# Moving the activation arena and the weight buffers of a float32r transformer kernel by 64 and 128 bytes in SBUF

## The chip, the cores and the metric

The kernel runs on one core of one Trainium2 chip. The metric is the device time of one execution in microseconds (us). The kernel before was timed three times: median 3365.83 us, lowest 3364.95, highest 3367.11.

## The reference

Two transformer layers follow each other on 256 tokens with a model width of 2048, in float32. The first has four mixers side by side (a gated delta rule, a linear recurrence, a spatial gating unit and a short convolution), then an output product and a feed-forward part with a convolution and GELU. The second has a SwiGLU, two kinds of attention with two branch products and an output product, and a second SwiGLU. Cut to the products with a large weight, which is where nearly all of the arithmetic lies:

```python
# first layer
p = h @ w_in                                   # 2048 -> 44 tiles of 128
y = concat(y_a, y_b, y_c, y_d) @ w_out         # 2048 -> 2048
hid = conv(h @ ffn_up); y = (gelu(gate) * val) @ ffn_down        # 2048 -> 11264, 5632 -> 2048
# second layer
x = x + 0.5 * swiglu(norm(x), w_gate, w_up, w_down)              # 2048 -> 2 x 5632, 5632 -> 2048
proj = norm(x) @ w_in_2                                          # 2048 -> 92 tiles of 128
y = sigmoid(g1) * (o_dil @ w_dil) + sigmoid(g2) * (o_diff @ w_diff)
x = x + y @ w_out_2
x = x + 0.5 * swiglu(norm(x), w_gate, w_up, w_down)
```

## The kernel before

Activations are held transposed: 128 channels on the partitions, 256 tokens along the free axis. A value is held as two halves in float32r, a high part and what is left over, side by side: one activation tile of halves is 2 x 256 elements of 4 bytes, 2048 bytes in each partition. Weights are streamed from memory in chunks of eight 128 x 128 tiles (`KG = 8`, 512 KB, 4096 bytes in each partition) through four slots (`SLOTS = 4`), and each chunk passes three buffers. SyncE's queue loads it into `weights_raw` (`load_chunk`, L266). ScalarE rounds it to `weights_high` (`split_high`, L306). VectorE subtracts that from the raw chunk into `weights_low` (`split_low`, L313). A tile of 128 weights columns is 512 bytes in a partition, and a slot is 4096 bytes.

TensorE then works in pairs of k tiles (`multiply_pair`, L463 and L466). For the two k of a pair it multiplies the high weights with both halves of the activation (512 columns), and after them, for the same two k, the low weights with the high half (256 columns). So the order of the weight loads and matmuls is high, high, low, low, without end, and every matmul has a weight load of its own (PEld in the profile), which runs while the matmul before it streams its activation. Within one product the activation tile moves by 2048 bytes from k to k, and the weight tile by 512. The last two tiles of some products go through `multiply_joined` (L478, L481), which takes the halves in two matmuls of 256 columns.

Which activation buffer a product reads depends on the product. `moving_halves` (over `halves_memory`) serves the input, up and gate products of both layers. `gated_halves` begins where the arena begins and serves the three down products. `gated_branch_halves` begins 28 x 1024 bytes into the arena (output product of the second layer), `branch_halves` 4 x 1024 bytes into it (branch products), and `mixed_halves` 4 x 44 x 260 = 45,760 bytes into it (output product of the first layer).

SBUF tensors are laid out one behind the other in the order in which `Core.__init__` asks for them (L150 to L175): `x_T`, `halves_memory`, a gap, `arena`, a gap, `weights_raw`, `weights_high`, `weights_low`, and then the small buffers. The gaps are tensors that nothing reads or writes. Starts are rounded up to 32 bytes, and the sizes named here are multiples of 32.

The engines run in step by semaphores alone: SyncE waits for `low_ready` before it overwrites a raw slot, ScalarE waits for the load and for TensorE to free the slot, VectorE for ScalarE, TensorE for VectorE. ScalarE, VectorE and GpSimd also take the finished accumulators, scale and activate them.

Of the kernel before, what the change touches and what calls it, by code (L numbers as in the profile page):

```python
# [10 lines left out]
F32 = mybir.dt.float32  # L11
# [6 lines left out]
P = 128  # L18
# [37 lines left out]
class Chain:  # L56


    def __init__(self, eng, sem):
        self.eng, self.sem, self.n = eng, sem, 0  # L60
# [84 lines left out]
class Core:  # L145


    def __init__(self, nc, ctx, d):
        self.nc, self.ctx, self.d = nc, ctx, d
        self.x = self.sb("x_T", [P, KT, S], F32)  # L150

        self.h_at = nc.sbuf_base
        self.x_at = self.h_at - KT * S * 4
        self.h_mem = self.sb("halves_memory", [P, KT, 2, S], F32)
        self.h = self.over(self.h_at, "moving_halves", KT)

        self.sb("before_arena", [P, 32], F32)
        self.arena_at = nc.sbuf_base
        self.arena = self.sb("arena", [P, ARENA_TILES, S], F32)
        self.g_parts = self.over(self.arena_at, "gated_halves", FF_TILES)  # L160
        self.y_parts = self.over(self.arena_at + 28 * S * 4, "gated_branch_halves", KT)
        self.sb("before_weights", [P, 48], F32)
        self.raw = self.sb("weights_raw", [P, SLOTS, KG * P], F32)
        self.high = self.sb("weights_high", [P, SLOTS, KG, P], F32R)
        self.low = self.sb("weights_low", [P, SLOTS, KG, P], F32R)
        self.cross = self.sb("cross_products", [P, 2, S], F32)
        self.z = self.sb("unscaled", [P, 2, S], F32)
        self.sq = self.sb("squares", [P, 2, S], F32)
        self.total = self.sb("squares_total", [P, S], F32)
        self.rs = self.sb("token_scale", [P, S], F32)  # L170
        self.trig = self.sb("trig", [ROPE, 2, S], F32)
        self.lam = self.sb("lam", [P, 3], F32)
        self.vec = self.sb("vectors", [P, N_VECTORS], F32)
        self.const = self.sb("constants", [P, N_CONSTS], F32)
        self.scratch = self.sb("stage_scratch", [P, SCRATCH], F32)  # L175
        self.acc = self.scale_bank = None
        self.first_loaded, self.rest_loaded = self.sem("first_loaded"), self.sem("rest_loaded")
        self.half_high, self.half_low = self.sem("half_high"), self.sem("half_low")
        self.loaded = [self.sem(f"weights_loaded{s}") for s in range(SLOTS)]
        self.x_loaded = [self.sem(f"x_loaded{g}") for g in range(KT // 4)]  # L180
        self.high_ready = self.sem("high_ready")
        self.low_ready = self.sem("low_ready")
        self.full_loaded = [self.sem(f"full_loaded{s}") for s in range(SLOTS)]
        self.full_used, self.full_ready = (self.sem(n) for n in ("full_used", "full_ready"))
        self.y_gained, self.squares_added = self.sem("y_gained"), self.sem("squares_added")
        self.fulls = 0
        self.slots_free = self.sem("slots_free")
        self.acc_free = self.sem("acc_free")
        self.cross_ready = self.sem("cross_ready")
        self.z_free, self.idle_in = self.sem("z_free"), self.sem("idle_in")  # L190
        self.y_scaled = self.sem("y_scaled")
        self.x_ready = self.sem("x_ready")
        self.part_high = self.sem("part_high")
        self.part_low = self.sem("part_low")
        self.squared = self.sem("squared")
        self.squares_used = self.sem("squares_used")
        self.summed = self.sem("summed")
        self.carried = self.sem("carried")
        self.var_ready = self.sem("var_ready")
        self.rooted = self.sem("rooted")  # L200
        self.newton = self.sem("newton")
        self.rs_ready = self.sem("rs_ready")
        self.hidden_free = self.sem("hidden_free")
        self.activated = self.sem("activated")
        self.product_ready = self.sem("product_ready")
        self.g_high = self.sem("g_high")
        self.g_low = self.sem("g_low")
        self.swiglus = 0
        self.pairs = 0
        self.halves = 0  # L210
        self.parts = 0
        self.squares = 0
        self.totals = 0
        self.norms = 0
        self.xs = 0
        self.ys = 0
        self.scaled = 0
        self.chunk = 0
        self.tile = 0
# [3034 lines left out]
```

## Time and profile before

| | |
|---|---|
| Median of three runs | 3365.83 us (3364.95 to 3367.11) |
| Profiled execution | 3365.98 us, span 3364.2 us |
| TensorE matmul (PE) busy | 3345.9 us, 99% |
| TensorE weight load (PEld) busy | 2933.9 us, 87% |
| VectorE (DVE) busy | 2240.1 us, 67% |
| ScalarE (ACT) busy | 1746.2 us, 52% |
| GpSimd (POOL) busy | 533.2 us, 16% |
| Memory traffic | 616.21 MB, mean 183 GB/s |
| Granted TensorE clock | 1.000 of 2.4 GHz |

Matmuls are pipelined and one begins long before the one ahead of it has ended, so a mean duration of 395 ns is no rate. The rate is read from starts: how far apart in time the same step of the loop begins again. Here that step is one pair of k tiles, four matmuls.

### The profile page before, as it was taken

Reading aid. Unit: us, or ns where it says so; the run is one execution under the profiler, and the core shown is the slowest. Engines: PE = TensorE matmul, PEld = TensorE weight load, DVE = VectorE, ACT = ScalarE, POOL = GpSimd, SP = SyncE. Lnnn points to the kernel's source line nnn. Section 1 sums busy time; section 2 is a strip of 40 time slices with the busy share of each in tenths; the row PEclk is TensorE's granted clock in tenths of the full one; section 3 lists DMA queues with packets and bytes.
Section 4 is the critical chain, followed back from the end, with each engine's and each line's share of the span. In section 5 each row is a group of like instructions: output and inputs, shape, how many; then the busy total and the mean of one; then the engine's idle time right before and its main releaser. Section 6 shows DMA issues by size and latency. Waiting matters only on the chain.

```text
span 3364.2 us, 59341 instructions
## 1 busy us (share of the span) xinstructions
PE 3345.9 (99%) x19746; PEld 2933.9 (87%) x19746; DVE 2240.1 (67%) x2874; ACT 1746.2 (52%) x2588; POOL 533.2 (16%) x502
## 2 busy tenths in 40 slices
PE   9999999999999999999999999999999999999999
PEld 8888888888888888888888888888888888888888
DVE  7879587777744566556555599766687655656544
ACT  5555665555544554545444555554565554554443
POOL 0214111111100011111100066511100111111000
PEclk9999999999999999999999999999999999999999
DMA  6534555555566555555566655545556555555665
GB/s 213 163 114 154 184 169 189 190 188 187 188 193 188 178 179 192 189 190 187 187 192 189 219 175 175 189 155 159 171 193 199 190 187 193 188 188 189 186 194 175
DMA packets 176036, 616.21 MB, mean 183 GB/s; under 512 B 20912, under 2 KB 21584, under 8 KB 175568
## 3 DMA queue, kind: packets, MB, share of 16 engines
q1 hardware_dynamic: 175520, 609.84, 56.2%
q10 hardware_dynamic: 432, 5.24, 0.4%
q8 instruction: 53, 0.87, 0.1%
q14 instruction: 31, 0.25, 0.0%
HBM read 610.81 MB, written 4.19 MB: 183 GB/s over the span
## 4 chain that ended last, share of the span: by engine, by line
PE 94%; DVE 3%; issue 1%; ACT 1%; DMA 1%; POOL 0%; DVEq 0%; SPq 0%; POOLq 0%; ACTq 0%
PE acc L463 59%; PE acc L466 30%; DVE weights_low L313 1%; PE ps_wide L392 1%; PE acc L478 1%; ACT weights_high L306 0%; PE ps_narrow L2552 0%; PE ps_wide L2528 0%; PE acc L481 0%; DVE halves_memory L568 0%; DMA weights_raw<-in_w_in 0%; DMA x_T<-in_x 0%; DVE halves_memory L3011 0%; DMA weights_raw<-in_w_diff_branch 0%; PE ps_scale L2933 0%
## 5 line engine op out<-in xcount | busy, mean ns | idle before, releaser
L463 PE MATMUL acc<-moving_halves,weights_high 128*128 128x512 f32 x6304 | 1981.0, 395 | 1.8 <-DVE x_T L2821 1.8
L313 DVE TENSOR_TENSOR weights_low<-weights_raw,weights_high 128x1024 fp32r<-128x1024 f32 (+1 forms) x1172 | 1432.8, 1236 | 719.8 <-ACT weights_high L306 718.6
L306 ACT ACTIVATE weights_high<-weights_raw 128x1024 fp32r<-128x1024 f32 (+1 forms) x1172 | 1209.0, 1033 | 773.1 <-PE acc L466 746.7
L466 PEld LDWEIGHTS acc<-moving_halves,weights_low 128*128 128x128 f32 x6304 | 1185.0, 188 | 269.0
L466 PE MATMUL acc<-moving_halves,weights_low 128*128 128x256 f32 x6304 | 1244.0, 279 | 0.0
L463 PEld LDWEIGHTS acc<-moving_halves,weights_high 128*128 128x128 f32 x6304 | 952.4, 188 | 12.0 <-issue 9.8
L463 PE MATMUL acc<-gated_halves,weights_high 128*128 128x512 f32 x2024 | 628.0, 392 | 0.0
L562 ACT ACTIVATE cross_products<-acc 128x256 f32<-128x256 f32 x503 | 192.9, 383 | 671.2 <-PE acc L466 671.1
L466 PEld LDWEIGHTS acc<-gated_halves,weights_low 128*128 128x128 f32 x2024 | 380.1, 188 | 83.8
L585 POOL TENSOR_TENSOR stage_scratch<-unscaled,token_scale 128x256 f32<-128x256 f32 x260 | 215.2, 828 | 1287.2 <-DVE unscaled L568 807.3
L466 PE MATMUL acc<-gated_halves,weights_low 128*128 128x256 f32 x2024 | 399.4, 279 | 0.0
L568 DVE TENSOR_TENSOR unscaled<-acc,cross_products 128x256 f32<-128x256 f32 x354 | 150.0, 424 | 274.5 <-ACT cross_products L562 274.3
L463 PEld LDWEIGHTS acc<-gated_halves,weights_high 128*128 128x128 f32 x2024 | 306.5, 188 | 0.0
L585 POOL TENSOR_TENSOR arena<-unscaled,token_scale 128x256 f32<-128x256 f32 (+1 forms) x74 | 71.7, 969 | 424.4 <-DVE unscaled L568 424.4
L622 POOL TENSOR_TENSOR squares_total<-squares_total,squares 128x256 f32<-128x256 f32 x56 | 42.4, 758 | 524.7 <-ACT squares L609 524.7
L1281 ACT ACTIVATE gated_halves<-stage_scratch 128x256 f32 (+1 forms) x88 | 36.8, 418 | 84.5 <-DVE stage_scratch L1314 84.5
L463 PE MATMUL acc<-gated_branch_halves,weights_high 128*128 128x512 f32 x256 | 79.4, 392 | 0.0
L1187 DVE SCALAR_TENSOR_TENSOR arena<-stage_scratch,vectors,arena 128x256 f32<-128x256 f32 x88 | 63.6, 723 | 21.8 <-ACT arena L1148 20.2
L463 PE MATMUL acc<-mixed_halves,weights_high 128*128 128x512 f32 x240 | 75.5, 396 | 0.3 <-DVE mixed_halves L1966 0.3
L2910 POOL TENSOR_TENSOR arena<-arena,trig 32x512 f32<-32x512 f32 x20 | 75.5, 3776 | 0.0
L463 PE MATMUL acc<-branch_halves,weights_high 128*128 128x512 f32 x192 | 61.3, 401 | 1.0 <-DVE halves_memory L568 0.7
L466 PEld LDWEIGHTS acc<-gated_branch_halves,weights_low 128*128 128x128 f32 x256 | 48.1, 188 | 10.5
(384 smaller groups left out, 2010.7 us busy)
## 6 DMA issues: line engine op xcount, KB each, us to landing
weights_raw<-in_w_in SPq DMA_DIRECT2D x268, 512.0 KB, 3.9
weights_raw<-in_ffn_up SPq DMA_DIRECT2D x176, 512.0 KB, 4.5
weights_raw<-in_ffn_w_gate SPq DMA_DIRECT2D x176, 512.0 KB, 4.1
weights_raw<-in_ffn_w_up SPq DMA_DIRECT2D x176, 512.0 KB, 4.7
weights_raw<-in_ffn_w_down SPq DMA_DIRECT2D x160, 512.0 KB, 4.0
weights_raw<-in_ffn_down SPq DMA_DIRECT2D x80, 512.0 KB, 4.0
weights_raw<-in_w_out SPq DMA_DIRECT2D x64, 512.0 KB, 4.3
weights_raw<-in_ffn_w_down SPq DMA_DIRECT2D x32, 256.0 KB, 2.7
```

What stands on the lines that cost most here:

```text
L306: core.nc.scalar.activation(core.high[:, slot, k0:nk, :].rearrange("p a b -> p (a b)"), core.raw[:, slot, k0 * P:nk * P], ACT.Copy).then_i ...
L313: core.nc.vector.tensor_tensor(core.low[:, slot, k0:nk, :].rearrange("p a b -> p (a b)"), core.raw[:, slot, k0 * P:nk * P], core.high[:, s ...
L392: last = core.nc.tensor.matmul(core.full_sums[:, t, 0:S], w, operand.full[:, k, :], start=(k == 0), stop=(k == KT - 1))
L463: core.nc.tensor.matmul(acc[:, t % 2, :, :], core.high[:, u % SLOTS, k, :], parts[:, prod.first[t] + k0 + k, :, :], start=(k0 + k == 0), s ...
L466: core.last = core.nc.tensor.matmul(acc[:, t % 2, 0, :], core.low[:, u % SLOTS, k, :], parts[:, prod.first[t] + k0 + k, 0, :], start=False ...
L562: core.nc.scalar.activation(core.cross[:, t % 2, :], acc[:, t % 2, 1, :], ACT.Copy).then_inc(core.cross_ready, 1)
L568: core.nc.vector.tensor_tensor(out, acc[:, t % 2, 0, :], core.cross[:, t % 2, :], ALU.add).then_inc(core.acc_free, 1)
L585: core.nc.gpsimd.tensor_tensor(out, core.z[:, t % 2, :], core.rs[:, :], ALU.mult).then_inc(core.z_free, 1)
L622: core.nc.gpsimd.tensor_tensor(core.total[:, :], core.total[:, :], core.sq[:, t % 2, :], ALU.add).then_inc(core.squares_used, 1)
L1187: nc.vector.scalar_tensor_tensor(conv[:, t, :], hidden[:, t, PAD - 1:PAD - 1 + S], tap(i, t, 1), conv[:, t, :], ALU.mult, ALU.add).then_in ...
L1281: nc.scalar.activation(g_parts[:, i, 0, :], g, ACT.Copy).then_inc(core.g_high, 1)
L2910: nc.gpsimd.tensor_tensor(here, here, each(trig[:, 0, :]), ALU.mult).then_inc(pool_own, 1)
```

## The change

The gap of 128 bytes ahead of the arena goes. The gap of 192 bytes ahead of the weight buffers stays. A gap of 192 bytes is put between `weights_high` and `weights_low`. No instruction is added, removed or moved in the program. By the order of the tensors, `arena`, `weights_raw` and `weights_high` start 128 bytes lower than before, and `weights_low` and all that follows it 64 bytes higher. `x_T` and `halves_memory` stay.

```diff
         self.h_mem = self.sb("halves_memory", [P, KT, 2, S], F32)
         self.h = self.over(self.h_at, "moving_halves", KT)
 
-        self.sb("before_arena", [P, 32], F32)
         self.arena_at = nc.sbuf_base
         self.arena = self.sb("arena", [P, ARENA_TILES, S], F32)
         self.g_parts = self.over(self.arena_at, "gated_halves", FF_TILES)
@@
         self.sb("before_weights", [P, 48], F32)
         self.raw = self.sb("weights_raw", [P, SLOTS, KG * P], F32)
         self.high = self.sb("weights_high", [P, SLOTS, KG, P], F32R)
+        self.sb("before_low", [P, 48], F32)
         self.low = self.sb("weights_low", [P, SLOTS, KG, P], F32R)
```

## Rows read from the trace of the kernel before

**Rows 1.** The page, part 1 (busy time by engine) and part 4 (chain).

```profile
PE 3345.9 (99%) x19746; PEld 2933.9 (87%) x19746; DVE 2240.1 (67%) x2874; ACT 1746.2 (52%) x2588; POOL 533.2 (16%) x502
...
PE 94%; DVE 3%; issue 1%; ACT 1%; DMA 1%; POOL 0%; DVEq 0%; SPq 0%; POOLq 0%; ACTq 0%
```

**Rows 2.** Waits of TensorE, longest first: total us, times, longest.

```profile
PE ps_narrow L2453 <- DVE stage_scratch L2425: 2.6, 1, 2.6
```

**Rows 3.** Groups of TensorE instructions, forms apart: count, busy us, mean ns, idle.

```profile
L463 PE MATMUL acc<-moving_halves,weights_high 128*128 128x512 f32 x6304 | 1981.0, 395 | 1.8 <-DVE x_T L2821 1.8
...
L463 PE MATMUL acc<-gated_halves,weights_high 128*128 128x512 f32 x2024 | 628.0, 392 | 0.0
...
L463 PE MATMUL acc<-gated_branch_halves,weights_high 128*128 128x512 f32 x256 | 79.4, 392 | 0.0
L463 PE MATMUL acc<-mixed_halves,weights_high 128*128 128x512 f32 x240 | 75.5, 396 | 0.3 <-DVE mixed_halves L1966 0.3
L463 PE MATMUL acc<-branch_halves,weights_high 128*128 128x512 f32 x192 | 61.3, 401 | 1.0 <-DVE halves_memory L568 0.7
```

**Rows 4.** Windows, PE with moving_halves: stretch, us, busy, matmuls, clock, DMA.

```profile
1200.00:1660.00 460.00, 460.00 (x2656) 1.00 0.57 189
```

**Rows 5.** The same with gated_halves alone.

```profile
3130.00:3330.00 200.00, 200.00 (x1162) 1.00 0.63 190
```

**Rows 6.** Timeline of a product with moving_halves: start us, length us.

```profile
1500.22 0.62 PE L463 MATMUL acc<-moving_halves,weights_high 128*128 128x512 f32 x2
...
1500.45 0.42 PEld L466 LDWEIGHTS acc<-moving_halves,weights_low 128*128 128x128 f32 x2
...
1500.69 0.39 PE L466 MATMUL acc<-moving_halves,weights_low 128*128 128x256 f32 x2
...
1500.81 0.30 PEld L463 LDWEIGHTS acc<-moving_halves,weights_high 128*128 128x128 f32 x2
...
1500.92 0.62 PE L463 MATMUL acc<-moving_halves,weights_high 128*128 128x512 f32 x2
```

**Rows 7.** Timeline of a product with gated_halves.

```profile
1000.25 0.62 PE L463 MATMUL acc<-gated_halves,weights_high 128*128 128x512 f32 x2
...
1000.49 0.42 PEld L466 LDWEIGHTS acc<-gated_halves,weights_low 128*128 128x128 f32 x2
...
1000.72 0.39 PE L466 MATMUL acc<-gated_halves,weights_low 128*128 128x256 f32 x2
...
1000.83 0.30 PEld L463 LDWEIGHTS acc<-gated_halves,weights_high 128*128 128x128 f32 x2
...
1000.94 0.62 PE L463 MATMUL acc<-gated_halves,weights_high 128*128 128x512 f32 x2
...
1001.17 0.42 PEld L466 LDWEIGHTS acc<-gated_halves,weights_low 128*128 128x128 f32 x2
...
1001.40 0.40 PE L466 MATMUL acc<-gated_halves,weights_low 128*128 128x256 f32 x2
...
1001.52 0.30 PEld L463 LDWEIGHTS acc<-gated_halves,weights_high 128*128 128x128 f32 x2
...
1001.63 0.62 PE L463 MATMUL acc<-gated_halves,weights_high 128*128 128x512 f32 x2
```

**Rows 8.** Timeline of the product with mixed_halves, three pairs of k apart.

```profile
400.33 0.63 PE L463 MATMUL acc<-mixed_halves,weights_high 128*128 128x512 f32 x2
...
402.42 0.63 PE L463 MATMUL acc<-mixed_halves,weights_high 128*128 128x512 f32 x2
```

**Rows 9.** All engines in an up product: busy us and count of PE, PEld, DVE, ACT, POOL.

```profile
1200.00:1660.00 460.00, 460.00 (x2656) 403.55 (x2655) 274.89 (x333) 229.19 (x332) 66.92 (x83) 1.00 0.57 189
```

**Rows 10.** Groups of instructions in the stretch 1200 to 1660 us.

```profile
L313 DVE TENSOR_TENSOR weights_low<-weights_raw,weights_high 128x1024 fp32r<-128x1024 f32 x167 | 212.8, 1291 | 114.3 <-ACT weights_high L306 114.3
...
L306 ACT ACTIVATE weights_high<-weights_raw 128x1024 fp32r<-128x1024 f32 x166 | 175.3, 1056 | 50.7 <-PE acc L466 47.0
```

## The prediction, before the changed kernel had run

> **What bounds the kernel now.** The page comes first: matmuls cover 99% of the span and TensorE holds 94% of the chain that ended last [rows 1]. The waits of TensorE come next: the longest in the whole run is 2.6 us, and it occurs once [rows 2]. So in the large products TensorE waits for no other engine, and the time is the number of matmuls by the distance between their starts. The groups of instructions give the number: 6304 matmuls of high weights read `moving_halves`, 2024 `gated_halves`, 256 `gated_branch_halves`, 192 `branch_halves` and 240 `mixed_halves` [rows 3]. Two of them, with their two of low weights, are one pair of k tiles, which I use as the unit: 3152 pairs with `moving_halves`, 1012 + 128 + 96 = 1236 with the three buffers that begin at the arena's start or a multiple of 512 bytes behind it, 120 with `mixed_halves`.
>
> Now the distance. With `moving_halves`, 460 us hold 2656 matmuls, about one and a half of them only cut by the edges (each is recorded as 390 ns long, and one starts every 173 ns): 460 / (2654.5 / 4) = 0.693 us for a pair [rows 4]. With `gated_halves`, 200 us hold 1162, or 1160.5 without the edges: 0.689 us, and the timeline gives 1.38 us for two pairs, 0.690 [rows 5, 7]. With `mixed_halves` three pairs take 2.09 us, 0.697 [rows 8]. The instructions are the same in the three cases, the shapes are the same, the clock is 1.00 in the rows that show it (the upper level, 2.4 GHz), and nothing waits. What differs is where in SBUF the activation tile lies against the weight tile. The pattern of starts repeats whether ScalarE and VectorE are busy or not, so I take the difference to lie between TensorE's own two reads: the activation that it streams and the weights that it loads for the next matmul at the same time (a PEld row begins together with a matmul in each gap [rows 6, 7]).
>
> **Distances.** Tiles move by multiples of 512 bytes in both streams, so what stays the same throughout a product is the distance modulo 512 from the activation tile to the weight tile. Before, from `moving_halves` to `weights_high`: 32,768 + 128 + 94,208 + 192 + 16,384 = 143,680, which is 320 modulo 512. From `gated_halves`: 94,208 + 192 + 16,384 = 110,784, which is 192 (also for the two branch buffers, whose offsets 28,672 and 4096 are multiples of 512). From `mixed_halves`: 110,784 - 45,760 = 65,024, which is 0. `weights_low` lies 16,384 further, so it has the same distance as the high weights in every product. The trace therefore holds three measured points: distance 320 gives 0.693, 192 gives 0.690, 0 gives 0.697.
>
> After: the 128 bytes go, so `moving_halves` has 192 to the high weights; `gated_halves` and its kin keep 192, since arena and high weights move together. `weights_low` is 192 further in all of them: 384. `mixed_halves` has 0 to the high and 192 to the low weights. So 4388 of the 4508 pairs will run in one and the same arrangement, high at 192 and low at 384, and have one pitch P. The change as a whole comes down to P.
>
> **Part 1: high weights.** At 192 they stand as with `gated_halves` now. A weight load of the high tile runs in the gap from the first high matmul to the second and in that from the second low one to the next high one. With `gated_halves` two pairs give 0.24 + 0.11 and 0.23 + 0.11, so 0.345 us for a pair. With `moving_halves` it is 0.23 + 0.11 = 0.34 [rows 6, 7]. Starts are read to 10 ns, so these halves are good to some 5 to 10 ns; their sum is exact by the windows.
>
> **Part 2: low weights.** They load in the gaps from high to low and from low to low: with `moving_halves` 0.24 + 0.12 = 0.36 us, with `gated_halves` 0.23 + 0.11 and 0.23 + 0.12, so 0.345 [rows 6, 7]. What `moving_halves` pays more than `gated_halves` thus lies with the low loads. Distance 384 isn't in the trace. I bound the half from both sides by the cheapest and the dearest half read: 0.34 and 0.36. I take 0.345, the low loads' own value with `gated_halves`, as it is also the nearest to the middle of what three of the four halves show (0.34, 0.345, 0.345). By distance alone the nearest point would be 320, which speaks for more, and this is the weak place of the sum.
>
> **Sum.** P = 0.345 + 0.345 = 0.690. `moving_halves`: 3152 x (0.690 - 0.693) = -10.1 us with the difference unrounded (460 / 663.6 = 0.6932). `gated_halves` and kin: 1236 x 0 = 0. `mixed_halves`: 120 pairs, high still at 0, low now at 192; half of 0.007 each, -0.4 us. Together -10.5 us on the profiled execution's 3365.98 us: 3355.5, so 3355 us. That execution lies 0.15 us from the median of the runs shown, so the same number stands for the median; 1.8 us of it lies outside the span, and the change doesn't touch it. The bounds of P are 0.34 + 0.345 = 0.685 and, above, 0.697, the dearest pitch that the trace has for a whole product. A nanosecond of P is 4.4 us of time, and the time stays as it is at P = 0.692.
>
> **What may move elsewhere, and is costed at nothing.** The raw, high and low buffers are also read and written by ScalarE, VectorE and the loads. In an up product ScalarE is busy 229 and VectorE 275 of 460 us [rows 9]; a split takes 1056 and 1291 ns, and VectorE's idles 114 us there for ScalarE, ScalarE's 47 us for TensorE [rows 10]. A chunk of eight k tiles comes every 4 x 0.693 = 2.8 us, so a split may grow by some 40% before TensorE would wait. If the cover were gone, each 100 ns by which a chunk is late would cost 0.1 us for each of 1172 chunks. The loads come with 0.57 of the DMA engines' time [rows 4], with nothing waiting for them. The stages between the products have under 6% of the chain [rows 1]; their operands move with the arena, and 1% more on all of them is 2 us. I set both at 0.
>
> The skill's rule speaks against the whole sum. The Trainium skill, "SBUF — State Buffer", section "Who interferes with whom", says that only the port pair shared by VectorE and GpSimd causes contention and that TensorE never waits for anyone, its two reads being independent. By that rule no layout could alter a pitch, and the time would stay at 3366 us. This case's trace disagrees: 0.690, 0.693 and 0.697 for the same instructions. A rule on the rate, in "TensorE: Matmul & The Clock Gate", section "Back-to-back issue gap", gives N / 2.4 + 2.5 ns for a matmul taken by itself; 2 x 215.8 + 2 x 109.2 is an estimate of 0.650 us for a pair, so some 40 ns of each pair would be left to win, far more than any distance in the trace has given back.
>
> **The rivals.**
>
> *Better than any row.* The low loads at 384 cost less than the cheapest half read, because high and low no longer meet the activation at the same distance and the delay of one doesn't carry into the other. For it: the pitch with `gated_halves` isn't even, low to low takes 0.68 us and then 0.70 [rows 7], so shorter pairs do occur. Against it: the three distances seen lie within 7 ns. At P = 0.685: 3152 x -8.2 ns = -26 us and 1236 x -5 ns = -6 us, so 3334 us; in this case values from 3325 to 3348.
>
> *Nothing in sum.* Low loads at 384 behave as those at their nearest row, 320, and take away what the high ones give: P = 0.691 to 0.694, which is -6 to +7 us; at 0.692, 3366 us. The same time comes if the layout has no effect of its own and the three pitches have another cause, such as the place in the loop over k; against that, all buffers go through the same loop.
>
> *Slower.* One mechanism: the low loads at 384 run into the stream as they do at 0, modulo 512 the other neighbour, where the whole product shows 0.697 [rows 8]. All down products then lose what they have now, and the up products lose too. At P = 0.696: 3152 x 2.8 = 8.8 us and 1236 x 6 = 7.4 us, so 3382 us. It decides from P = 0.694 on. For it: 384 lies between 320 and 512, the two dearer of the three points. Against it: the low loads' half at 0 isn't known to be the dear one.
>
> **How the numbers follow.** What a measurement of this kernel can tell from no change is about 0.2%, 6.7 us. Forecast (P about 0.690, its own range 3348 to 3360): 0.33. Better than any row: 0.22. Nothing in sum: 0.21, the layout without effect among it. Slower: 0.24. So faster by over 0.2% has 0.33 + 0.22 = 0.55, less 0.01 for values of the forecast near the edge, 0.54; same 0.22; slower 0.24. The range goes from 3332 us, which leaves out a third of the better case (0.08), to 3380 us, which leaves out half of the slower one (0.12).
>
> **What would show it.** In the profile after, counts of instructions and waits are as before, and the pitch of the up and down products is one and the same number; that is the step on which all rests. If the up and down products still differ, the distance modulo 512 isn't what counts. If both show 0.690, part 2 is right; if they agree on another number, part 2 is mis-sized and the time follows at 4.4 us for a nanosecond. If the high loads' gaps (first high to second high, low to high) with `moving_halves` don't come to 0.345, part 1 is wrong. The prediction as a whole is wrong if TensorE's waits grow or if splits take a different time and the matmuls wait for them.

## The result and the profile after

The changed kernel takes 3410.18 us (median of four runs, 3409.53 to 3411.21) against 3365.61 us for the kernel before in the same comparison: a ratio of 1.0129, 95% interval 1.0116 to 1.0143. It is slower by 44.6 us. The forecast was 3355 us, faster, with a range up to 3380 us. Direction and range are both missed.

The page after has the same counts of instructions and the same chain as before [rows 1]; what has grown with the span is TensorE's busy time, by 49 us for the matmuls and 25 us for the weight loads.

```profile
span 3409.4 us, 59341 instructions
PE 3394.8 (100%) x19746; PEld 2958.5 (87%) x19746; DVE 2243.0 (66%) x2874; ACT 1745.1 (51%) x2588; POOL 532.3 (16%) x502
PE 94%; DVE 3%; issue 1%; ACT 1%; DMA 1%; POOL 0%; DVEq 0%; SPq 0%; POOLq 0%; ACTq 0%
```

TensorE's longest wait in the run after is even shorter than the one of before [rows 2]:

```profile
PE acc L463 <- DVE x_T L2821: 1.6, 1, 1.6
```

The windows give the pitch, here with the matmuls on `moving_halves` alone (stretch, us, busy us, matmuls, granted clock, DMA share, GB/s). About one and a half matmuls of each count are cut by the edges, so the pitch of a pair of k tiles is length x 4 / (count - 1.5), as in [rows 4]:

```profile
500.00:900.00 400.00, 400.00 (x2267) 1.00 0.57 186
1250.00:1650.00 400.00, 400.00 (x2277) 1.00 0.58 186
```

That is 0.706 us in the first layer's up product and 0.703 in the second layer's first one, where [rows 4] had 0.693. With `gated_halves`, where [rows 5] had 0.689 and [rows 7] 0.690, the first, the third and the second down product, in this order:

```profile
960.00:1140.00 180.00, 180.00 (x1021) 1.00 0.63 185
...
3190.00:3360.00 170.00, 170.00 (x969) 1.00 0.64 187
1710.00:1890.00 180.00, 180.00 (x1026) 1.00 0.60 184
```

In the order of the rows that is 0.706, 0.703 and 0.703. Up and down products now have the same two values, the granted clock stays at 1.00, and the matmuls only begin further apart. The product with `mixed_halves` went the same way. Two rows of it, four pairs apart:

```profile
399.81 0.63 PE L463 MATMUL acc<-mixed_halves,weights_high 128*128 128x512 f32 x2
...
402.64 0.63 PE L463 MATMUL acc<-mixed_halves,weights_high 128*128 128x512 f32 x2
```

That is 2.83 us for four pairs. The mean over all 120 pairs of this product is 0.706 us, where the trace before has 0.697. The timeline of the second up product, beside [rows 6]:

```profile
1299.65 0.63 PE L463 MATMUL acc<-moving_halves,weights_high 128*128 128x512 f32 x2
1299.88 0.42 PEld L466 LDWEIGHTS acc<-moving_halves,weights_low 128*128 128x128 f32 x2
1300.12 0.40 PE L466 MATMUL acc<-moving_halves,weights_low 128*128 128x256 f32 x2
1300.23 0.30 PEld L463 LDWEIGHTS acc<-moving_halves,weights_high 128*128 128x128 f32 x2
1300.35 0.64 PE L463 MATMUL acc<-moving_halves,weights_high 128*128 128x512 f32 x2
1300.59 0.43 PEld L466 LDWEIGHTS acc<-moving_halves,weights_low 128*128 128x128 f32 x2
1300.82 0.40 PE L466 MATMUL acc<-moving_halves,weights_low 128*128 128x256 f32 x2
1300.94 0.31 PEld L463 LDWEIGHTS acc<-moving_halves,weights_high 128*128 128x128 f32 x2
1301.06 0.62 PE L463 MATMUL acc<-moving_halves,weights_high 128*128 128x512 f32 x2
```

The two pairs take 1.41 us. The low loads' gaps (high to low and low to low) are 0.24 + 0.11 and 0.23 + 0.12, the high loads' 0.23 + 0.12 and 0.24 + 0.12: 0.35 and 0.355 us for a pair, each good to 5 to 10 ns. The starts that the trace holds, averaged over the 680 pairs of this product, are sharper: 0.355 us for the low loads' gaps and 0.349 for the high loads'. The same averages before are 0.354 and 0.339 with `moving_halves` and 0.347 and 0.343 with `gated_halves`. So not the low loads alone are slower, the high ones are too.

Where the 45.2 us of span went, from these pitches: 688 pairs in the first up product at 13 ns more are 9 us, 688 + 704 in the other two at 10 ns 14 us, 1012 pairs with `gated_halves` at 13 to 16 ns 14 us, 128 with `gated_branch_halves` 2 us. Together 39 us. The remaining 6 us lie elsewhere. By the starts of the products in the two traces, 1 us stands ahead of the product with `mixed_halves`, 1 us in it, and 4 us between the second down product and the output product of the second layer.

The splits, as ScalarE's rounding and VectorE's subtraction are called here, didn't change. In the second up product (beside [rows 10]):

```profile
L313 DVE TENSOR_TENSOR weights_low<-weights_raw,weights_high 128x1024 fp32r<-128x1024 f32 x143 | 183.7, 1291 | 99.4 <-ACT weights_high L306 99.4
...
L306 ACT ACTIVATE weights_high<-weights_raw 128x1024 fp32r<-128x1024 f32 x142 | 149.6, 1054 | 46.1 <-PE acc L466 41.2
```

VectorE's takes 1291 ns in both, ScalarE's 1054 against 1056.

### The profile page after: what moved, and what is told of

It reads as the page before. It is cut to its first block, busy times and chain, and to the rows that moved or that the text cites. A ratio compares the mean times of both kernels' runs of the same rounds, so it can differ in the third digit from the quotient of the medians.

```text
span 3409.4 us, 59341 instructions
## 1 busy us (share of the span) xinstructions
PE 3394.8 (100%) x19746; PEld 2958.5 (87%) x19746; DVE 2243.0 (66%) x2874; ACT 1745.1 (51%) x2588; POOL 532.3 (16%) x502
## 4 chain that ended last, share of the span: by engine, by line
PE 94%; DVE 3%; issue 1%; ACT 1%; DMA 1%; POOL 0%; DVEq 0%; SPq 0%; POOLq 0%; ACTq 0%
PE acc L463 59%; PE acc L466 30%; DVE weights_low L313 1%; PE ps_wide L392 1%; PE acc L478 1%; ACT weights_high L306 0%; PE ps_narrow L2552 0%; PE ps_wide L2528 0%; PE acc L481 0%; DVE halves_memory L568 0%; DMA weights_raw<-in_w_in 0%; DMA weights_raw<-in_w_diff_branch 0%; DVE halves_memory L3011 0%; DMA x_T<-in_x 0%; PE ps_wide L2539 0%
## 5 line engine op out<-in xcount | busy, mean ns | idle before, releaser
L466 PE MATMUL acc<-moving_halves,weights_low 128*128 128x256 f32 x6304 | 1261.8, 281 | 0.0
L463 PEld LDWEIGHTS acc<-moving_halves,weights_high 128*128 128x128 f32 x6304 | 965.8, 188 | 10.6 <-issue 7.9
L463 PE MATMUL acc<-gated_halves,weights_high 128*128 128x512 f32 x2024 | 636.7, 396 | 0.0
```

Source lines behind the costliest of these rows:

```text
L463: core.nc.tensor.matmul(acc[:, t % 2, :, :], core.high[:, u % SLOTS, k, :], parts[:, prod.first[t] + k0 + k, :, :], start=(k0 + k == 0), s ...
L466: core.last = core.nc.tensor.matmul(acc[:, t % 2, 0, :], core.low[:, u % SLOTS, k, :], parts[:, prod.first[t] + k0 + k, 0, :], start=False ...
```

## The experiments

Distances are given as (high, low): from the activation tile to the tile of `weights_high` and to that of `weights_low`, modulo 512 unless said otherwise. Pitches come by windows of 400 us in the second up product (`moving_halves`) and of 120 us in the first down product (`gated_halves`), which are good to about 1 ns; where another product of the same run differs, the text says so. Each edit is shown against the kernel that the text names. Line numbers are shifted by one where a kernel has one gap fewer or more. Apart from the first, each experiment has one run, and runs of one kernel lie up to 5 us apart, so the pitches carry the argument.

**The arena's part alone.** The kernel before without its gap ahead of the arena: both weight tiles at 192 for `moving_halves` and `gated_halves`.

```diff
-        self.sb("before_arena", [P, 32], F32)
```

> The arena's gap is gone, weights_low stays directly behind weights_high: both weight tiles 192 bytes (modulo 512) behind the activation tile in every product but the mixed one. Theory D (the distances modulo 512 from the activation tile to the high and to the low tile set the pitch): 0.690 us for a pair of k tiles with moving_halves as well as with gated_halves, so 3152 x 3.2 ns = 10 us less than before, about 3355 us; the low tile's distance 384 is then the whole cause of the slower pitch. Rival A (the arena's or the high weights' own address is what hurts): moving_halves at 0.70 or more, time near 3400 us.

Measured: 3357.06 us (3354.42 to 3359.26, 8 runs) against 3366.08, a ratio of 0.9973, interval 0.9962 to 0.9984. Windows with `moving_halves`, then with `gated_halves`:

```profile
1250.00:1650.00 400.00, 400.00 (x2321) 1.00 0.59 190
```

```profile
1000.00:1120.00 120.00, 120.00 (x698) 1.00 0.64 189
```

0.690 and 0.689 us. Theory D holds for this part, and the time is 2 us from the 3355 expected, so with both weight tiles at 192 the forecast pitch comes out, and the whole loss comes with the gap ahead of `weights_low`. This layout beats both kernels.

**The low buffer's part alone.** The changed kernel with the gap ahead of the arena put back: (192, 384) for `gated_halves`, (320, 0) for `moving_halves`.

```diff
+        self.sb("before_arena", [P, 32], F32)
```

> The arena's gap stays and the 192 bytes ahead of weights_low are added. Theory D: gated_halves has the distances of the changed kernel (192 and 384), so its pitch is 0.704 us; moving_halves has 320 and 0, not seen yet, between 0.690 and 0.710. Time between 3372 and 3435 us. Rival S (the distance between the high and the low buffer matters, through the engines that write them): both products at 0.704, about 3415 us. Rival A (arena's position): gated_halves back near 0.690.

Measured: 3432.11 us (one run). `moving_halves`, then `gated_halves`:

```profile
1250.00:1650.00 400.00, 400.00 (x2245) 1.00 0.57 184
```

```profile
1000.00:1120.00 120.00, 120.00 (x684) 1.00 0.63 189
```

`gated_halves` has 0.703, as D says; the arena's place is not the cause, which drops rival A. `moving_halves` has 0.713, the slowest pitch of an up or down product in any run: just outside the 0.710 expected, and not the 0.704 that rival S gave it.

**Everything moved together.** The changed kernel with 192 bytes ahead of `x_T`.

```diff
+        self.sb("before_x", [P, 48], F32)
         self.x = self.sb("x_T", [P, KT, S], F32)
```

> The changed kernel with 192 bytes more ahead of x_T, so that everything moves up together and all distances stay. Theory D: 0.704 us for a pair in both kinds of product, 3410 us. Rival A (absolute addresses modulo 512 or 1024 count): another pitch, 0.690 to 0.70, and a time 10 us or more from 3410.

Measured: 3408.05 us (one run).

```profile
1250.00:1650.00 400.00, 400.00 (x2277) 1.00 0.57 186
```

The same count as after, 0.703 us, so for this product the move changes nothing. Two other products are not as after. The first up product has the same row here, 0.703, where the changed kernel has 0.706:

```profile
500.00:900.00 400.00, 400.00 (x2277) 1.00 0.57 187
```

With `mixed_halves`, at (0, 192) in both, four pairs take 2.77 us, where the changed kernel has 2.83:

```profile
399.72 0.62 PE L464 MATMUL acc<-mixed_halves,weights_high 128*128 128x512 f32 x2
...
402.49 0.62 PE L464 MATMUL acc<-mixed_halves,weights_high 128*128 128x512 f32 x2
```

The kernel of the experiment before this one has (0, 192) there too, and also 2.77 us for four pairs. The means over the whole product are 0.694 in both and 0.706 in the changed kernel. So distances decide most of it, but not all.

**Equal distances elsewhere.** Two kernels made from the kernel before put high and low weights at other distances, the same for both. The first:

```diff
-        self.sb("before_arena", [P, 32], F32)
+        self.sb("before_arena", [P, 16], F32)
...
-        self.sb("before_weights", [P, 48], F32)
+        self.sb("before_weights", [P, 16], F32)
```

> Gaps of 64 bytes ahead of the arena and of 64 ahead of the weights, none ahead of weights_low: high and low both at distance 128 for moving_halves, 64 for gated_halves, 384 for mixed_halves. Theory D with 384 as the bad distance for any weight tile: mixed_halves slower than its 0.697, at 0.705 or more. Rival M (high and low at unequal distances are what costs, 384 by itself isn't bad): mixed_halves at 0.690 to 0.697. For 128 and 64 no forecast better than 0.690 to 0.705; a modulus of 256 in place of 512 would give 64 the pitch of 320, 0.693.

Measured: 3379.80 us (one run). The product with `mixed_halves`, which has both tiles at 384 here:

```profile
402.35 0.62 PE L463 MATMUL acc<-mixed_halves,weights_high 128*128 128x512 f32 x2
...
405.13 0.62 PE L463 MATMUL acc<-mixed_halves,weights_high 128*128 128x512 f32 x2
```

Four pairs in 2.78 us, 0.695 to 0.697 with the rounding of starts, no slower than in [rows 8]. Distance 384 isn't bad by itself; rival M stands and the other reading of D falls. The other two points, `moving_halves` at 128 and `gated_halves` at 64:

```profile
1250.00:1650.00 400.00, 400.00 (x2299) 1.00 0.58 188
```

```profile
1000.00:1120.00 120.00, 120.00 (x695) 1.00 0.64 190
```

0.696 and 0.692. The value at 64 is, within 1 ns, that of 320 in [rows 4], and the value at 384 that of 128. That suggested a modulus of 256, which the next kernel put to the test with `gated_halves` at 256, `moving_halves` at 448 and `mixed_halves` at 64:

```diff
-        self.sb("before_arena", [P, 32], F32)
+        self.sb("before_arena", [P, 48], F32)
...
-        self.sb("before_weights", [P, 48], F32)
+        self.sb("before_weights", [P, 64], F32)
```

> Gaps of 192 bytes ahead of the arena and 256 ahead of the weights, none ahead of weights_low: high and low at equal distance, 256 for gated_halves, 448 for moving_halves, 64 for mixed_halves. Theory E (with equal distances, only the distance modulo 256 counts; so far 320 and 64 gave 0.693, 0, 128 and 384 gave 0.697, 192 gave 0.690): gated_halves 0.697, moving_halves 0.690, mixed_halves 0.693, sum 3165 us for moving, 1236 x 6.7 ns more for gated: about 3364 us. Rival (modulus 512): other pitches, anywhere in 0.685 to 0.71.

Measured: 3366.78 us (one run), where 3364 was expected.

```profile
1250.00:1650.00 400.00, 400.00 (x2320) 1.00 0.58 190
```

```profile
1000.00:1120.00 120.00, 120.00 (x691) 1.00 0.63 188
```

0.690 and 0.696 us, within 1 ns of the forecasts. The third, 0.693 with `mixed_halves` at 64, holds too, with 2.77 us for four pairs, 0.694 in the mean:

```profile
399.78 0.62 PE L463 MATMUL acc<-mixed_halves,weights_high 128*128 128x512 f32 x2
...
402.55 0.62 PE L463 MATMUL acc<-mixed_halves,weights_high 128*128 128x512 f32 x2
```

(The 3165 us in the expectation's sum doesn't fit its total: 3355 with the 8 us for `gated_halves` is the 3364 it ends on.) With equal distances in steps of 64 the pitch goes by the distance modulo 256: 0.690 at 192, 0.693 at 64, 0.697 at 0 and 128.

**The size of the gap ahead of the low buffer.** First 256 in place of 192 in the changed kernel.

```diff
-        self.sb("before_low", [P, 48], F32)
+        self.sb("before_low", [P, 64], F32)
```

> The changed kernel with 256 bytes ahead of weights_low in place of 192: high at 192, low at 448 modulo 512. Theory E with modulus 256: high and low are equal again, 0.690 in both kinds of product, 3355 us. Rival (modulus 512, or any gap between high and low costs): 0.700 or more, 3400 us.

Measured: 3355.73 us (one run).

```profile
1250.00:1650.00 400.00, 400.00 (x2321) 1.00 0.58 190
```

```profile
1000.00:1120.00 120.00, 120.00 (x698) 1.00 0.64 189
```

64 bytes more give back all that the change lost and what its first part wins. A gap of 256 bytes ahead of `weights_low` is free. The small buffers behind `weights_low` move too when the gap changes, and here they don't cost anything. Then 64 and 128 bytes in the kernel before:

```diff
         self.high = self.sb("weights_high", [P, SLOTS, KG, P], F32R)
+        self.sb("before_low", [P, 16], F32)
```

> The kernel before with 64 bytes ahead of weights_low: low 64 further than high in every product. Theory U (any shift between high and low that isn't a multiple of 256 costs, as each change of buffer makes the phase of weight reads jump): 0.700 to 0.715 in both, about 3410 us. Rival V (the shift of 192 is bad by its sign or size, others can be good): one of the products at 0.690 or below.

Measured: 3392.18 us (one run), `moving_halves` at 0.700 and `gated_halves`, just below the range of theory U, at 0.697:

```profile
1250.00:1650.00 400.00, 400.00 (x2288) 1.00 0.58 187
```

```profile
1000.00:1120.00 120.00, 120.00 (x690) 1.00 0.63 188
```

```diff
         self.high = self.sb("weights_high", [P, SLOTS, KG, P], F32R)
+        self.sb("before_low", [P, 32], F32)
```

> The kernel before with 128 bytes ahead of weights_low. Theory U: 0.700 to 0.715 in both products, about 3410 us. Rival V: at least one product at 0.690 or below, 3355 us or less.

Measured: 3368.72 us (one run). `moving_halves` is as in the kernel before; the second row is `gated_halves`, and the third has all matmuls of a stretch of the output product on `gated_branch_halves`:

```profile
1250.00:1650.00 400.00, 400.00 (x2310) 1.00 0.58 189
```

```profile
1000.00:1120.00 120.00, 120.00 (x694) 1.00 0.64 189
```

```profile
2560.00:2640.00 80.00, 80.00 (x457) 1.00 0.60 188
```

0.693, 0.693 and 0.703 us. Theory U as I had put it, that any shift other than a multiple of 256 costs 10 ns or more, is wrong at 128: there the up products keep 0.693 and the down products go from 0.690 to 0.693. Rival V is wrong too, since none is at 0.690 or below. In the up and down products shifts of 64 and 192 bytes cost 7 to 20 ns, and 128 costs 0 to 3. Beside them only the second layer's output product is slow, at the same distances, (192, 320), as `gated_halves`.

**Steps of 32 bytes.** Again the kernel before, with other gaps:

```diff
-        self.sb("before_arena", [P, 32], F32)
+        self.sb("before_arena", [P, 48], F32)
...
-        self.sb("before_weights", [P, 48], F32)
+        self.sb("before_weights", [P, 56], F32)
```

> Gaps of 192 bytes ahead of the arena and 224 ahead of the weights, none ahead of weights_low: high and low at equal distance, 224 for gated_halves, 160 (modulo 256) for moving_halves, 32 for mixed_halves. Theory E (equal distances, modulus 256) gives no value for steps of 32; if the pitch goes smoothly, 224 lies between 192 (0.690) and 0 (0.697), so 0.693, 160 between 128 (0.697) and 192 (0.690), so 0.693, and 32 at 0.695: about 3368 us. Rival (what counts is the 64-byte line, a start that isn't on one costs more): over 0.700 in all, 3400 us or more. Rival (a half line off is the best place): below 0.690.

Measured: 3402.03 us (one run). `moving_halves` at 160, `gated_halves` at 224:

```profile
1250.00:1650.00 400.00, 400.00 (x2287) 1.00 0.57 187
```

```profile
1000.00:1120.00 120.00, 120.00 (x694) 1.00 0.63 188
```

0.700 and 0.693 in these two. Other products of the same run differ at the same distances: the first up product, and the output product with `gated_branch_halves`, which is at 224 as well:

```profile
500.00:900.00 400.00, 400.00 (x2266) 1.00 0.56 185
```

```profile
2570.00:2650.00 80.00, 80.00 (x454) 1.00 0.59 188
```

Both have 0.707. So at 160 the pitch is 0.700 or 0.707, at 224 it is 0.693 or 0.707, and the smooth course holds only for 224, and there only in the down products. No product is below 0.690, which drops the second rival; the first one's "over 0.700 in all" fails at 224. Neither reading of 32-byte steps covers both.

**Who disturbs the reads.** The low matmuls take their weights from `weights_high`; the product with the low weights is left out, everything else, the small buffers behind `weights_low` too, is as in the changed kernel.

```diff
-        core.last = core.nc.tensor.matmul(acc[:, t % 2, 0, :], core.low[:, u % SLOTS, k, :],
+        core.last = core.nc.tensor.matmul(acc[:, t % 2, 0, :], core.high[:, u % SLOTS, k, :],
```

> The changed kernel in which the low matmuls take their weights from weights_high instead of weights_low: the product with the low weights is left out in this way, while ScalarE and VectorE still write both buffers where the change put them. Theory D/U (TensorE's own two reads against each other, with the jump between the buffers as the cost): TensorE now reads weights only at distance 192, so 0.690 and about 3355 us. Rival S (the engines that write at the shifted address slow TensorE's reads): 0.704 and 3410 us.

Measured: 3357.00 us (one run). The loads of weights that TensorE makes and the matmuls are as many as after, and VectorE still writes the shifted low buffer. All PE matmuls in an up product and a down product:

```profile
1250.00:1650.00 400.00, 400.00 (x2321) 1.00 0.59 190
1000.00:1120.00 120.00, 120.00 (x698) 1.00 0.63 191
```

0.690 and 0.689. The writers don't matter, rival S is out: the cost lies between TensorE's own reads. The trace after says the same. In its first up product a pair takes 0.707 us in the mean both where the two splits run nearly all through it (36 pairs) and where hardly any of either does (106 pairs).

**Fewer changes between the buffers.** Four high and four low matmuls in turn, first in the changed kernel, then in the layout of the first experiment.

```diff
-        for pair in range(0, nk, 2):
-            (multiply_joined if joined else multiply_pair)(core, prod, acc, t, u, pair, k0, before)
+        for pair in range(0, nk, 2 if joined else 4):
+            if joined:
+                multiply_joined(core, prod, acc, t, u, pair, k0, before)
+            else:
+                multiply_pair(core, prod, acc, t, u, pair, k0, before, 4)
...
-    ks = range(pair, min(pair + 2, nk))
+    ks = range(pair, min(pair + many, nk))
```

> The changed kernel with four high matmuls and then four low ones, in place of two and two, in the part of multiply() that most bodies use: half as many changes between the two weight buffers. Theory U (the cost of unequal distances is paid at each change of buffer): the 14 ns over 0.690 halve, 0.697 us for a pair, about 3379 us. Rival W (each low load pays by its own distance, however it is ordered): 0.704, 3410 us.

Measured: 3394.30 us (one run).

```profile
1250.00:1650.00 400.00, 400.00 (x2287) 1.00 0.57 187
```

> The layout without the arena's gap and without a gap ahead of weights_low (high and low both at 192), with four and four. Theory U: no jump in phase at a change of buffer, so 0.690 as with two and two, about 3356 us. Rival (the change between 512 and 256 columns costs by itself): 0.680 to 0.687, 3315 to 3345 us.

Measured: 3363.56 us (one run).

```profile
1250.00:1650.00 400.00, 400.00 (x2315) 1.00 0.59 190
```

0.700 and 0.692 us. With two and two the shifted layout stands 13 ns over the even one (0.703 and 0.690), with four and four 8 ns; in the times it is 53 us and 31 us. Halving the changes leaves 31 / 53 = 0.58 of the cost by time and 8 / 13 = 0.62 by pitch, where U says 0.5 and rival W 1. So W, which forecast no gain, is out, and fewer changes of buffer make the cost smaller, if less than U says. That it is paid at the changes isn't shown. By the mean gaps of the traces, four high and four low matmuls take 17 ns more in the shifted layout than in the even one, and only 6 of them lie in the two gaps where the buffer changes; either the delay is carried on from there, or it arises elsewhere. The even layout loses 7 us by four and four where U forecast no change and the rival a gain, so no gain from fewer switches between 512 and 256 columns showed.

## Why the prediction was wrong, point by point

**What bounds the kernel.** Right. Waits, splits and counts are as before, and at least 39 of the 45 us are pitch.

**Distances decide, and up and down products get one pitch.** Right in the main: the two kinds of product agree, at 0.703 or 0.706 in both, and the writers have no effect. But one arrangement isn't one pitch, as the prediction took for granted. The 0.706 of the first up product is gone when everything is moved together, and `mixed_halves`, which was to gain 0.4 us, lost 1 us in the changed kernel (0.706) and, at the same distances, gains 0.4 us in the moved one (0.694). The modulus was wrong, 256 and not 512. For the change this had no consequence, since none of its distances falls on another by it, but it puts 384 on 128 and 192 + 256 on 192, and would have shown that the three rows of the trace were three of four points.

**Part 1, high weights at 192.** Right where it stands alone: the first experiment has -9.0 us in the direct comparison, where the sum had -10.1 us for `moving_halves`, and the high loads' gaps there are 0.343 us by the trace's mean. In the changed kernel it isn't: the high loads' gaps came to 0.349 us in the second up product, not 0.345, although high weights and activation lie as in the first experiment. By the sign that the prediction set for this part it is wrong there, and for the reason that part 2 fails.

**Part 2, low weights at 384.** This is the step that failed. The half was taken as 0.345 us within 0.34 to 0.36, and the high half was held at 0.345, so P = 0.690 with 0.697 as its upper bound. Measured are 0.355 us for the low half and 0.349 for the high one, by the means of the second up product, and a P of 0.703 to 0.706. Not the size of one half is off but the sum's form. I added what high loads cost at their distance and low loads at theirs, as if each gap stood alone. The runs show that the two don't add: both tiles at 384 give 0.697, both at 192 give 0.690, and high at 192 with low at 384 gives more than either, 0.703. Even the gap from high to high, in which both reads belong to distance 192, grew from 0.227 us in the first experiment to 0.232 in the changed kernel. All points of the trace before had the two at the same distance, so a difference between them was not an unknown between measured ends but a new quantity, and the ends taken from those rows were no bounds. The upper bound was also narrower than the prediction's own halves allow: with 0.36 for the low half P is 0.345 + 0.36 = 0.705, which is 3422 us by its sum, but it took 0.697, the dearest whole product, and ended the range at 3380. The time follows: 13 ns over the forecast pitch at 4.4 us for a nanosecond is 57 us, against 3410 - 3355 = 55.

**The slower rival** had the right sign and the wrong mechanism, the closeness of 384 to 0: with both tiles at 384 the pitch was 0.695 to 0.697. Its price of 3382 us rested on the same rows, so its ceiling was the same. That the cost of a gap depends on the gap before was written under the better rival, with its sign reversed.

**The rule of the Trainium skill** that TensorE waits for no one ("SBUF — State Buffer", section "Who interferes with whom") would have given 3366 us. The runs disagree further than the trace of before did: the same matmuls and loads at 0.690 to 0.713 us by the layout alone. The kernel that reads the high weights twice fits the rule in so far as the writers indeed don't disturb TensorE; its two reads disturb each other.

**What stays open.** How the memory is divided so that this comes out was not settled. The experiments give the pitch for sixteen pairs of distances modulo 256, not the rule behind it: why a shift of 128 costs little and 64 or 192 more, why 160 is slow and 224 only in one product, what chooses between the two pitches that some arrangements have, and why no layout comes near 0.650 us. That last is only an estimate, from the Trainium skill's figure for a matmul by itself ("TensorE: Matmul & The Clock Gate", section "Back-to-back issue gap"), and the best pitch measured is 0.690.

## What to carry to other kernels

Where matmuls with a weight load each run back to back and TensorE waits for no other engine, the starts of the buffers can be worth up to 3% of the pitch (0.690 to 0.713 us here): read the distance between starts in each product, and compare products that differ in their buffers alone. Keep alternating weight buffers at the same offset modulo 256 bytes from the activations, and then try the four offsets in steps of 64; here 192 was the best, and no unequal pair came below 0.693. All of this was measured with tiles that lie multiples of 512 bytes apart, and nothing shows it for others. And where all measured points share a property that the change breaks, take no bound from them: the range has to be wider than they are.

## What the runs showed that was not expected

One and the same arrangement can run at two pitches in one execution. In the changed kernel the first up product holds 0.706 us and the second 0.703 throughout, at the same distances and even the same addresses; with both tiles at 160 it is 0.707 and 0.700. With 128 bytes ahead of the low buffer, `gated_branch_halves` is at 0.703 and `gated_halves` at 0.693. So a pitch read from one product need not hold for another at the same distances, and the pattern of delays seems to be one that the two reads settle into and keep until something interrupts them; that is a reading of these rows, no run was made to show it.

A layout that costs nothing to build gives 3357 us: the kernel before without its 128 bytes ahead of the arena, 0.27% faster (interval 0.16% to 0.38%).
